# A hybrid transformer layer on one core: a new order for the scan's products and the attention's pieces in the second tile

## The reference

```python
def hybrid_layer(x, c, ...):
    h = rms_norm(x, norm1_g) * (1.0 + scale1) + shift1
    proj = h @ w_in                                  # 1824 columns for the scan, 1536 for attention
    y_rwkv = rwkv7_time_mix(proj[..., :RWKV_PROJ], ...)
    y_moba = moba_attention(proj[..., RWKV_PROJ:], q_norm_g, k_norm_g)
    x = x + gate1 * (jnp.concatenate([y_rwkv, y_moba], axis=-1) @ w_out)
    h = rms_norm(x, norm2_g) * (1.0 + scale2) + shift2
    y = moe_ffn(h.reshape(B * S, D), ...)            # 32 experts, the best 4 for each token
    return x + gate2 * y.reshape(B, S, D)
```

## Time and profile before

| what | value |
|---|---|
| median of 3 runs | 1932.95 us (1931.88 to 1934.26) |
| the profiled execution: its time, its span | 1932.87 us, 1931.1 us |
| TensorE (PE) busy | 1717.9 us, 89% |
| VectorE (DVE), ScalarE (ACT), GpSimd (POOL) busy | 48%, 24%, 15% |
| mean granted TensorE clock | 0.933 |
| HBM read | 770.53 MB, 400 GB/s over the span |

### The profile page before, as it was taken

The page is one execution under the profiler, slowest core; times in us unless marked ns, Lnnn a source line. Parts: engine busy times, 40 slices in busy tenths (PEclk is TensorE's granted clock), DMA queues, the critical chain, the costliest instruction groups (busy, mean ns, idle before and its releaser), DMA issues.

```text
span 1931.1 us, 28350 instructions
## 1 busy us (share of the span) xinstructions
PE 1717.9 (89%) x11370; PEld 804.8 (42%) x11370; DVE 920.0 (48%) x2002; ACT 468.2 (24%) x1184; POOL 292.7 (15%) x286
## 2 busy tenths in 40 slices
PE   9999997667679877878989999999999999999998
PEld 7888554211135523425873333333333333333332
DVE  4755978788664766554542322232232223223222
ACT  1011434333344533443221111111011111101101
POOL 1001443343433354350000000000000000000000
PEclk9999998776679989888999999999999999999999
DMA  9993999999999999999668999999999999999997
GB/s 391 382 412 112 417 421 420 421 421 422 420 421 420 418 409 420 421 420 370 268 258 375 428 427 428 426 427 428 429 427 427 428 429 427 427 428 429 427 429 302
DMA packets 81723, 773.00 MB, mean 400 GB/s; under 512 B 9076, under 2 KB 9332, under 8 KB 10200
## 3 DMA queue, kind: packets, MB, share of 16 engines
q1 hardware_dynamic: 44064, 500.50, 61.8%
q0 software_dynamic: 36864, 268.45, 33.5%
q10 hardware_dynamic: 696, 2.66, 0.4%
HBM read 770.53 MB, written 1.05 MB: 400 GB/s over the span
## 4 chain that ended last, share of the span: by engine, by line
PE 42%; DVE 5%; DMA 4%; issue 2%; ACT 0%; DVEq 0%; SPq 0%
PE psum L2474 21%; PE psum L2505 11%; PE psum L2517 3%; DMA arena<-in_w_gate_up 2%; DMA ring<-in_w_gate_up 2%; PE psum L2185 1%; PE psum L2488 1%; DVE arena L1835 1%; DVE arena L1838 1%; DVE arena L1832 1%; DVE arena L1833 1%; PE psum L2084 1%; PE psum L2460 1%; PE psum L2409 0%; PE psum L2369 0%
## 5 line engine op out<-in xcount | busy, mean ns | idle before, releaser
L2049 PE MATMUL psum<-ring,arena 64*64 64x512 f32 x1584 | 270.4, 765 | 113.5 <-ACT arena L927 112.0
L1411 DVE CUSTOM_DVE_ANT_0 ring<-ring,arena 128x1024 f32<-128x1024 f32 x198 | 241.0, 1224 | 117.2 <-DMA ring<-in_expert_uv,arena 109.0
L2474 PE MATMUL psum<-ring,arena 128*64 128x512 f32 x1248 | 275.3, 594 | 1.5 <-DMA ring<-in_w_gate_up 1.5
L791 POOL DMA_INDIRECT ring<-in_expert_uv,arena x198 | 218.7, 1104 | 310.2 <-PE psum L2049 284.6
L1832 DVE TENSOR_SCALAR arena<-psum 128x512 f32<-128x512 f32 x32 | 22.1, 692 | 370.8 <-PE psum L2474 370.8
L1121 ACT ACTIVATE arena<-arena 128x512 f32<-128x512 f32 x32 | 20.2, 630 | 728.4 <-DVE arena L1832 728.4
L2474 PE MATMUL psum<-arena 128*64 128x512 f32 x768 | 171.0, 594 | 2.8 <-DMA arena<-in_w_gate_up 2.1
L2474 PEld LDWEIGHTS psum<-ring,arena 128*64 128x64 f32 x1248 | 87.8, 137 | 183.9 <-issue 179.1
L2049 PEld LDWEIGHTS psum<-ring,arena 64*64 64x64 f32 x1584 | 52.0, 155 | 267.0 <-ACT arena L927 243.9
L2505 PE MATMUL psum<-ring,arena 128*64 128x512 f32 x560 | 125.1, 595 | 0.0
L918 ACT ACTIVATE late<-late 128x1 f32<-128x1 f32 x256 | 51.6, 201 | 295.6 <-DVE late L1411 292.0
(11 more groups left out here) (378 smaller groups left out, 1975.1 us busy)
## 6 DMA issues: line engine op xcount, KB each, us to landing
ring<-in_w_gate_up SPq DMA_DIRECT2D x78, 2048.0 KB, 24.6
arena<-in_w_gate_up SPq DMA_DIRECT2D x48, 2048.0 KB, 26.7
ring<-in_stream SPq DMA_DIRECT2D x91, 1024.0 KB, 13.8
ring<-in_w_down SPq DMA_DIRECT2D x35, 2048.0 KB, 25.6
arena<-in_w_down SPq DMA_DIRECT2D x28, 2048.0 KB, 22.5
gates_mats<-in_w_gate_up SPq DMA_DIRECT2D x2, 2048.0 KB
ring<-in_expert_uv,arena POOLq DMA_INDIRECT x198
gates_mats<-in_w_down SPq DMA_DIRECT2D x1, 2048.0 KB
```

Of the source, the lines that this page charges most:

```text
L791: pool.indirect_dma_start(rows_of[b].rearrange("p u d -> p (u d)"), None, expert_uv, bass.IndirectOffsetOnAxis(peer_i[:, tt, k:k + 1], 0)) ...
L1411: dve.tensor_tensor_reduce(u, u, h2[tt], 1.0, 0.0, ALU.mult, ALU.add, peer_h[:, tt, k:k + 1]).then_inc(dot_done, 1)
L2049: last = pe.matmul(psum[o:o + 64, 6 * tt + h, :], diag[rows, c % 4, :], rows_of[b][rows, 1, h * 512:(h + 1) * 512], start=(k == 0), stop=( ...
L2474: last = pe.matmul(psum[CAP * h:CAP * h + CAP, gu, :], x, w[:, at:at + 512], start=False, stop=(kt == GU_CHUNKS - 1), skip_group_check=True)
```

## The change

Only the list `ORDER` is edited; its set of stages stays the same. Within the second tile, the third half-piece of queries and keys (`mb1.0`) and all that follow it move behind one more stage of the scan each.

```diff
--- before.py
+++ after.py
@@ -206,9 +206,9 @@
 
 
 ORDER = """sum norm gain norm1 xn turn xres more rw0.0 rw0.1 rw1.0 rw1.1 mixl rw2.0 rw2.1 loin rw3.0 lora rw3.1 sigw mixk scan rw4.0 rw4.1 ksum kn
-rw5.0 rw5.1 exps mixr kmod rw6.0 rw6.1 rkk rw7.0 bonus rw7.1 mixv gup kk mb0.0 mb0.1 tilde mb1.0 mb1.1 bon gram0 nt tok3 mb2.0 gram1 mb2.1 pow1
-mb3.0 msq0 pow2 mb3.1 msq1 pow3 tok0 tok1 msum rms mb4.0 pow4 qk mb4.1 mscore0 soft0 pow5 tok2 mb5.0 mscore1 exp0 soft1 z1
-mb5.1 exp1 wu prob0 fg0 fg1 mturn0 prob1 fg2 fg3 mturn1 phi0 phi1 st0 aff st1 att st2 q2 yp om0 st3 ys om1 ln2 om2 om3 ln3
+rw5.0 rw5.1 exps mixr kmod rw6.0 rw6.1 rkk rw7.0 bonus rw7.1 mixv gup kk mb0.0 mb0.1 tilde bon gram0 nt tok3 mb1.0 gram1 mb1.1 pow1
+mb2.0 pow2 mb2.1 pow3 mb3.0 msq0 tok0 tok1 mb3.1 msq1 pow4 msum rms mb4.0 pow5 tok2 qk mb4.1 mscore0 soft0 z1 mb5.0 mscore1 exp0 soft1 wu
+mb5.1 exp1 fg0 prob0 fg1 mturn0 fg2 prob1 fg3 mturn1 phi0 phi1 st0 aff st1 att st2 q2 yp om0 st3 ys om1 ln2 om2 om3 ln3
 or0 or1 or2 or3 tn0 tn1 norm2 route""".split()
 RANK = {s: i for i, s in enumerate(ORDER)}
 
```

## The result

The changed kernel takes 1936.2 us in the median of 10 runs (1935.31 to 1941.9) against 1933.31 for the kernel before: 1.0018 times as long, with a 95% interval of 1.001 to 1.0026. It is slower by some 3.5 us by that ratio (2.9 by the two medians) where 1.9 us less was forecast, and it lies 1.6 us above the top of the range, 1934.6.

A forecast was written before the change was run, and what follows sets the result against it. TensorE's second-tile stretch was taken to reach the end one to one, only its holes being winnable: -6.82 + 3.1 (new waits) + 0.3 (broken runs) + 1.5 (fetches) = -1.9, so 1931.0 us, range 1928.4 to 1934.6.

The forecast's parts named there:

- the term for the fetches in the new order: TensorE's reordered stretch: two short instruction blocks make it wait for code, 0.2 plus 1.3, 1.5 us in sum.
- The block entered in gram0: First Gram product, entered at 934.4, used up in 3.4 us: successor's lateness put at 0.2, possible 0 to 2.7.
- The block entered in fg0: Entered about 969.6, used up in 3.6 us: successor's lateness put at the middle, 1.3, possible 0 to 2.5.
- The block in between: Between the two short blocks: counted among most blocks, lasting over 4.6 us, so no wait was added.
- rival 2: Late fetches in gram1 and fg3 cost 4.5 us against 3.4 won, plus 1.1: slower, 1934.0; chance 0.13.
- The four new waits: TensorE at tok3, the sums of squares, fg0 and after fg1: 0.7, 0.5, 0.8 and 1.0, together 3.0 to 3.1.
- The cut runs: First four halves of queries and keys, cut at two more places: 2 x 0.15 to 0.20, cost 0.3.
- The clock term: Low clock around 986.0 to 989.5: a shift may spare or add 1.3 us; 0 in the sum, 1.3 on both ends.
- Rival 1: Instruction fetches stay hidden in the reordered stretch: 3.4 us won, 1929.5, or 1928.2 with full clock; chance 0.25.
- Rival 3: Last 15 us of the stretch: softmax chain is the true bound, holes 1 to 2 us larger, 1932.9; chance 0.17.
- (c): fg0 directly after mb5.1 waits for the copy of values, 0.58, and two handovers: 0.8 us.
- (d): After fg0 and fg1, TensorE waits for the second exponentials and division, behind the copy of values: 1.0 us.

The follow-up runs named there:

- the fastest one: Changed kernel plus 24 idle 32 x 32 products (96 instructions) on TensorE, with three loads of experts' weights held back; 1927.11 us, 0.9966 of the kernel before.
- whole-block control: Changed kernel plus 256 idle instructions, a whole block, on TensorE during the wait for the second tile's normalisation; 1936.31 us, 1.0013 of the kernel before.
- 24 products: Changed kernel plus 24 idle 32 x 32 products (96 instructions) during the wait for the second tile's normalisation; 1930.95 us, 0.9984 of the kernel before.
- the first part alone: Kernel before with only the change up to pow3 (Gram products between the halves), all from pow4 on as before; 1937.53 us, 1.0019 of the kernel before.

## Why the prediction was wrong

**The step that failed** is the term for the fetches in the new order, "Sum 1.5, ends 0 and 5.2". It measured 5.76 us. Its three parts:

- *The block entered in gram0, taken at 0.2 and measured at 2.35.* The step said that "before, a block was entered at nearly the same moment, 934.2, behind the same traffic", and took that block's quick arrival as the price. Much the same traffic (a load issued 8.1 us earlier here, 7.9 there) gave 3.6 us from entering the block to its packet this time and 1.0 the other: 2.35 us of hole. The same hole was 0.63 and 1.25 us in two other kernels whose border lies there. One row was read as a constant where it varies from kernel to kernel; the two slow cases, 6.1 and 5.4 us, were in the same text. Holding back the load that was issued at 927 removed the hole, so the wait comes from the loads, whatever its size in one kernel.
- *The block entered in fg0, taken at 1.3.* It measured 2.55 us, at the upper end of 2.5: the load issued at 973.11 was ahead of it, as in the kernel before.
- *The block in between, taken at 0.* "Most blocks last over 4.6 us" is right, but 4.6 is not above 5.5: 0.86 us. With 6.1 as the upper bound this one had to be in the sum.

With the slow case for all, 2.7 + 1.5 + 2.5, the sum would have been 3.3 above the kernel before. That was rival 2, at 0.13: its place (gram1 and fg3) and its price for the two (4.5; measured 4.90) are what happened. The rival had the third fetch only as a way to need "still more", so its 1934.0 was short as well. Its chance was too small, and the range ended at 1934.6 although the prediction's own sum of the bad ends came to 1936.0.

**What was right.** The reading of the holes as late code, the size of a block and the borders (shifted by 96, 192 and 256 instructions, the holes moved as counted, and a hole in L2355 that had not been forecast lies on the grid too). The four new waits, 3.1 forecast and 2.90 measured, and the vanishing of the three of before. The cut runs, 0.3: a half between small products takes 1.98 us from its start to the next start (936.21 to 938.19) and 1.81 within its own kind, 0.17 for each of two. That what the stretch wins or loses reaches the end: +3.2 us in it, +4.7 at the first expert product with the 0.94 that was there before, +5.1 at the end; here the hole of 1.94 behind the stretch was not foreseen. The clock term: no net effect in this pair, but it is part of the gain of the kernels with held loads. Busy time of 980 to 1020 us, first of the kernel before and then of the fastest one:

```profile
980.00:1020.00 40.00, 37.72 (x452) 27.92 (x452) 14.63 (x46) 9.49 (x16) 0.00 (x0) 0.87 0.83 324
```

```profile
980.00:1020.00 40.00, 37.73 (x446) 26.32 (x444) 14.10 (x42) 9.50 (x16) 0.00 (x0) 1.00 0.81 317
```

It has the full clock throughout, where before was at 0.87. In these two traces the low level had cost the kernel before about 4.5 us, and the holes without a releaser had come to 5.83 us against 1.81, so clock and code have about equal shares; how the median's 6 us divide was not separated.

**Rival 1, hidden fetches**, fell. The page "Runtime: NRT & Kernel Launch" of the Trainium skill says in "Instruction fetch mechanics" that the fetch runs while the present block is executed and is mostly hidden, by the pace of issue. By that rule no hole would move when a load of weights is held back, and the whole-block control would be no different from 24 products. Here a block of small products goes by in 1.6 us (L2318) to 3.9 us (from fg0 on) and the three late ones of the changed kernel took 5.5 to 6.4 us beside weight loads: the measurement decides. **Rival 3**, larger waits in the softmax chain, fell with (c) and (d) at 0.77 and 0.91.

What stays open is why a fetch meets much the same loads once with 1.0 us and once with 3.6. In the two other kernels with that border in gram0 it was 1.9 (the first part alone) and 2.4 (the whole block), with the holes 0.63 and 1.25.

## What to carry to other kernels

If TensorE stops in the middle of a run of equal small products with no releaser, look for a packet on the instruction queue in that hole or just ahead of it (here it began 2.2 to 2.9 us before the work resumed); then count the instructions back and compute how fast each block of 256 goes by. An order is not judged by its own waits alone: with the borders elsewhere, the order that was 3.5 us slower became 2 us faster than the old one, and the old one, shifted alike, gained as much. Where large loads have slack, hold them until the dense part has its code; and measure two placements of the borders for each order before a reordering is judged.

## What was not expected of the hardware

- In the thirteen traces TensorE has 38 such holes of 0.3 us and more between 928 and 1010 us. From the first record of the block ahead to the resumed work it was 3.9 to 6.7 us where weights were being loaded ahead of the packet, and 2.0 to 3.9 in the four holes where none were.
- The packet of 16 KB itself takes about a microsecond, and from its start to the resumed work it was 2.2 to 2.9 us in all 38, loads or not. What the loads change is the time ahead of the packet: up to 1.2 us after the first record without them, 1.5 to 4.5 with them.
- 24 useless products in a wait were worth 5 us to the changed kernel, 64 of them nothing.
